# Both key heads of a local-attention block in one unit, and a start from half-width pieces of x, in a two-layer hybrid encoder trunk

## What is computed

```python
h = rms_norm(x, norm_mix)
z = h @ w_in                 # idx/latent, kv, bq, za, zd and 4 x 1024 gate columns
ya = gmlp_mixer(gelu(za))    # A: chunked spatial gating
yb = swa_sink_mixer(...)     # B: 8 query heads on 2 key heads, chunks of 64, window 128, sinks
yc = dsa_mixer(...)          # C: 4 heads over the 64 best keys of an index score
yd = pool_mixer(zd)          # D: causal means over 2, 4, 8, 16 tokens
merged = sum(sigmoid(zg[b]) * (y_b @ w_out[b]) for b in "ABCD")
x = x + merged @ w_o
h2 = rms_norm(x, norm_ffn)
x = x + (silu(h2 @ w_gate) * (h2 @ w_up)) @ w_down
```

## Time and profile before

| | us |
|---|---|
| median of 3 runs | 815.37 (814.8 to 815.8) |
| the profiled execution, its own time | 815.81 |
| its span, first to last instruction | 814.0 |
| PE busy | 805.4 |
| PE weight loads busy | 659.2 |
| DVE busy | 560.1 |
| ACT busy | 405.3 |
| POOL busy | 52.8 |

### The profile page before, as it was taken

The page is one execution under the profiler, slowest core; times in us unless marked ns, Lnnn a source line. Parts: engine busy times, 40 slices in busy tenths (PEclk is TensorE's granted clock), DMA queues, the critical chain, the costliest instruction groups (busy, mean ns, idle before and its releaser), DMA issues.

```text
span 814.0 us, 10244 instructions
## 1 busy us (share of the span) xinstructions
PE 805.4 (99%) x3868; PEld 659.2 (81%) x3868; DVE 560.1 (69%) x844; ACT 405.3 (50%) x558; POOL 52.8 (6%) x103
## 2 busy tenths in 40 slices
PE   7999999999999999999999999999999999999998
PEld 6888777878888888888888887787788888888886
DVE  6898789876576554565568887898675754565443
ACT  6866556454274434444366654755543543444431
POOL 5750000000000000000004100000000000000000
PEclk8999999999999999999999999999999999999999
DMA  8644536635466564665663625474446555666541
GB/s 300 215 147 145 173 135 207 207 127 188 135 223 201 177 191 158 207 205 184 177 218 120 230 82 182 133 252 158 155 155 206 180 183 165 209 196 195 167 155 52
DMA packets 98672, 144.38 MB, mean 177 GB/s; under 512 B 11064, under 2 KB 62016, under 8 KB 98624
## 3 DMA queue, kind: packets, MB, share of 16 engines
q1 hardware_dynamic: 98352, 143.73, 54.2%
q10 hardware_dynamic: 272, 0.00, 0.0%
HBM read 142.54 MB, written 1.05 MB: 176 GB/s over the span
## 4 chain that ended last, share of the span: by engine, by line
PE 95%; SPq 3%; DMA 1%; DVE 0%; ACT 0%; issue 0%; DVEq 0%
PE big L1504 20%; PE big L1508 19%; PE big L1507 19%; PE mix L1508 10%; PE mix L1504 10%; PE mix L1507 10%; SPq L581 2%; PE mix L1873 1%; PE mix L1548 1%; PE mix L1639 1%; DMA w_raw<-in_w_in 1%; PE mix L1572 1%; SPq L526 1%; PE mix L1560 1%; PE mix L1592 1%; PE mix L1625 1%
## 5 line engine op out<-in xcount | busy, mean ns | idle before, releaser
L731 ACT ACTIVATE w_hi<-w_raw 128x2048 fp32r<-128x2048 f32 (+3 forms) x142 | 256.6, 1814 | 163.2 <-DMA w_raw<-in_w_gate_up 88.3
L1032 DVE TENSOR_TENSOR w_lo<-w_raw,w_hi 128x2048 fp32r<-128x2048 f32 (+3 forms) x142 | 306.1, 2172 | 32.9 <-ACT w_hi L731 31.8
L1504 PE MATMUL big<-w_hi,act_hi 128*128 128x512 f32 (+2 forms) x476 | 185.6, 390 | 0.3 <-DVE w_lo L1032 0.3
L1507 PE MATMUL big<-w_lo,act_hi 128*128 128x512 f32 (+2 forms) x476 | 181.7, 382 | 0.0
L1508 PE MATMUL big<-w_hi,act_lo 128*128 128x512 f32 (+2 forms) x476 | 181.6, 382 | 0.0
L1504 PE MATMUL mix<-w_hi,act_hi 128*128 128x512 f32 x352 | 137.5, 391 | 0.0
L1508 PE MATMUL mix<-w_hi,act_lo 128*128 128x512 f32 x352 | 137.2, 390 | 0.0
L1507 PE MATMUL mix<-w_lo,act_hi 128*128 128x512 f32 x352 | 137.1, 389 | 0.0
L1504 PEld LDWEIGHTS big<-w_hi,act_hi 128*128 128x128 f32 x476 | 89.5, 188 | 20.1 <-issue 2.1
L1291 DVE TENSOR_TENSOR y_h_lo<-mix,y_h_hi 128x256 fp32r<-128x256 f32 x44 | 16.6, 419 | 127.4 <-ACT y_h_hi L950 127.4
L1508 PEld LDWEIGHTS big<-w_hi,act_lo 128*128 128x128 f32 x476 | 89.5, 188 | 17.2
(11 more groups left out here) (207 smaller groups left out, 717.2 us busy)
## 6 DMA issues: line engine op xcount, KB each, us to landing
w_raw<-in_w_in SPq DMA_DIRECT2D x44, 1024.0 KB, 5.1
w_raw<-in_w_gate_up SPq DMA_DIRECT2D x88, 512.0 KB, 4.8
w_raw<-in_w_down SPq DMA_DIRECT2D x22, 1024.0 KB, 4.9
w_raw<-in_w_o SPq DMA_DIRECT2D x8, 1024.0 KB, 5.0
w_raw<-in_b_w_out SPq DMA_DIRECT2D x4, 1024.0 KB, 5.9
w_raw<-in_w_in SPq DMA_DIRECT2D x3, 904.0 KB, 4.9
w_raw<-in_w_in SPq DMA_DIRECT2D x4, 512.0 KB, 4.3
w_raw<-in_a_w_out SPq DMA_DIRECT2D x4, 512.0 KB, 3.5
```

What stands on the lines that cost most here:

```text
L731: nc.scalar.activation(high(u)[:, a:b], arrived(u)[:, a:b], ACT.Copy).then_inc(hi_ready, 1)
L1032: nc.vector.tensor_tensor(low(u)[:, a:b], arrived(u)[:, a:b], high(u)[:, a:b].bitcast(F32), ALU.subtract).then_inc(lo_ready, 1)
L1504: ins = nc.tensor.matmul(dst[:, 0:w], xh, wh, start=first and n == 0, stop=False)
L1507: nc.tensor.matmul(dst[:, 0:w], xh, wl, start=False, stop=False)
```

## The change

**Attention.** `ATTN` has four units: B by token block with both key heads, and C by token block. Each unit of B writes 512 columns of each of two score banks where it wrote 256, reduces 1024 scores a row with one instruction, has eight exponentials, and two banks of transposes. `row` is 8 wide, `weights_b` is a view of `probs` with eight heads. In the tables the scores of the first unit move to slot 14, their transposes to 16; the index scores of block 1 move to slot 13 on PE and ACT (DVE's part stays in slot 15), TC to 16 with bank 0, TJ to 17. On DVE softmax_out and softmax_in come ahead of the ydT lows. The sinks are loaded by four DMAs instead of two.

**Start.** x is loaded in four pieces of 128 x 512; unit 1 in two halves as unit 0; the positions by SP. VectorE makes the high part of the first half of units 0 and 1 (`split_high`); ScalarE makes the high activations from PSUM with the gain as its scale (`first_gained`, four instructions of 128x128 for a piece) and VectorE the low ones (`first_low`, four more). Two more products of zeros stand behind the first transposes. The squares of x and their mean move behind slot 1's splits.

```diff
-ATTN = [("B", 0, 0), ("B", 0, 1), ("B", 1, 0), ("B", 1, 1), ("C", 0, 0), ("C", 0, 1)]
+ATTN = [("B", 0), ("B", 1), ("C", 0), ("C", 1)]
...
-    return 1 if ATTN[i][0] == "B" else ATTN[i][2] + 1
+    return 2 if ATTN[i][0] == "B" else ATTN[i][1] + 1
...
-PE_AT = {"latT": 5, "TI": 5, "kv": 7, "wT": 9, "TK": 8, "idx0": 10, "TQ": 11, "idx1": 14, "TC": 15, "TJ": 16,
+PE_AT = {"latT": 5, "TI": 5, "kv": 7, "wT": 9, "TK": 8, "idx0": 10, "TQ": 11, "idx1": 13, "TC": 16, "TJ": 17,
...
-S_AT = [13, 15, 17, 19, 23, 25]
-T_AT = [15, 17, 19, 21, 25, 27]
-Y_AT = [17, 19, 21, 23, 26, 28]
+S_AT = [14, 18, 23, 25]
+T_AT = [16, 20, 25, 27]
+Y_AT = [18, 23, 26, 28]
...
-            def load_tokens(tb):
-                sp.dma_start(xs[:, tb], x[0, tok(tb)]).then_inc(x_in[tb], 16)
+            def load_positions():
+                sp.dma_start(pos_i[:], positions[0].rearrange("(t p) -> p t", p=P),
+                             allow_slow_non_contiguous=True).then_inc(pos_in, 16)
+
+            def load_tokens(tb, h):
+                cols = slice(h * N, (h + 1) * N)
+                sp.dma_start(xs[:, tb, cols], x[0, tok(tb), cols]).then_inc(x_in[tb][h], 16)
...
-                if (l, u) == (0, 0):
+                if l == 0 and u < HALVED:
                     for half, k in ((0, slice(0, 2)), (1, slice(2, 4))):
...
-                        if half == 0:
-                            load_tokens(1)
+                        if (u, half) == (0, 0):
+                            load_tokens(1, 0)
+                        elif (u, half) == (0, 1):
+                            for tb in range(TB):
+                                load_tokens(tb, 1)
+                            load_positions()
...
-                    *((sinks[HD * a:HD * a + HD], b_sinks[l].rearrange("(k a o) -> a k o", k=2, a=2)[a].partition_broadcast(HD))
-                      for a in range(2)),
+                    *((sinks[HD * a:HD * a + HD, o],
+                       b_sinks[l].rearrange("(k a o) -> a o k", k=2, a=2)[a, o].partition_broadcast(HD))
+                      for a in range(2) for o in range(2)),
...
+            def first_gained(tb, h):
+
+                bank = mix_bank("hT", tb, h)
+                act.wait_ge(*mix_is_full(0, "hT", tb, h))
+                for j in range(4):
+                    k = 4 * h + j
+                    e = nc.scalar.activation(act_hi[:, k, tok(tb)], mix[:, bank, j * P:(j + 1) * P], ACT.Copy,
+                                             scale=g_mix[:, k:k + 1])
+                e.then_inc(act_hi_ready.sem, 1)
...
-                    load_positions()
-                    split(0, 0, 0)
-                    high_gained(0, "hT", 0)
+                    act.wait_ge(gain_placed, 1)
+                    first_gained(0, 0)
                     split(0, 0, 1)
-                    high_gained(0, "hT", 1, [0])
-                    x_squares(0, "mix", 0)
-                    split(0, 1, 0)
+                    first_gained(1, 0)
+                    first_gained(0, 1)
+                    first_gained(1, 1)
                     split(0, 1, 1)
-                    high_gained(0, "hT", 1, [1])
-                    x_squares(0, "mix", 1)
...
                     if (l, s) == (0, 1):
+                        for tb in range(TB):
+                            x_squares(0, "mix", tb)
                         tables()
...
+            def first_low(tb, h):
+                bank = mix_bank("hT", tb, h)
+                dve.wait_ge(*act_hi_ready.nth(0, 2 * h + tb + 1))
+                for j in range(4):
+                    k = 4 * h + j
+                    ins = nc.vector.scalar_tensor_tensor(
+                        out=act_lo[:, k, tok(tb)], in0=mix[:, bank, j * P:(j + 1) * P], scalar=g_mix[:, k:k + 1],
+                        in1=act_hi[:, k, tok(tb)].bitcast(F32), op0=ALU.mult, op1=ALU.subtract)
+                ins.then_inc(act_lo_ready.sem, 1)
+                dve.wait_ge(*gained_low(0, "hT", tb, h)).then_inc(mix_drained[bank].sem, 1)
+
+            def split_high(u):
+                dve.wait_ge(first_in[u], 16)
+                nc.vector.tensor_copy(high(u)[:, 0:2], arrived(u)[:, 0:2]).then_inc(first_high, 1)
...
-                    step(l, nc.vector.tensor_reduce(r0, s_in, AX_X, ALU.max))
+                    step(l, nc.vector.tensor_reduce(row[:, 0, :], s_in, AX_X, ALU.max))
...
+                for i in range(len(ATTN)):
+                    if s == T_AT[i] - 1:
+                        softmax_out(l, i)
+                for i in range(len(ATTN)):
+                    if s == S_AT[i]:
+                        softmax_in(l, i)
                 if s == PE_AT["ydT"]:
...
-                    gain_half(0, "hT", 0, 0)
-                    gain_half(0, "hT", 0, 1)
+                    split_high(0)
                     split(0, 0, 0)
-                    gain_low(0, "hT", 0, 0)
-                    gain_half(0, "hT", 1, 0)
+                    first_low(0, 0)
                     split(0, 0, 1)
-                    gain_low(0, "hT", 1, 0)
-                    gain_low(0, "hT", 0, 1)
-                    gain_half(0, "hT", 1, 1)
+                    first_low(1, 0)
+                    split_high(1)
                     split(0, 1, 0)
-                    gain_low(0, "hT", 1, 1)
+                    first_low(0, 1)
+                    first_low(1, 1)
                     split(0, 1, 1)
...
+                    if (l, s) == (0, 1):
+                        mean_of_sums(0, "mix", D_MODEL)
...
-                    turn(l, "hT", 0)
+                    turn(l, "hT", 0, [0])
+                    products_of_zeros(2)
                     first_products(0, 0)
-                    turn(l, "hT", 1)
-                    for half, kind in ((0, 1), (0, 2), (1, 0), (1, 1), (1, 2)):
+                    turn(l, "hT", 1, [0])
+                    for half, kind in ((0, 1), (1, 0), (0, 2), (1, 2), (1, 1)):
                         first_products(half, kind)
+                    for tb in range(TB):
+                        turn(l, "hT", tb, [1])
```

More of the change, by code:

```diff
@@ L154, in mixer_uses @@
              (("TQ", 0), 2), (("TQ", 1), 3), (("spatial",), 1), (("mixed",), 2),
-             (("yaT",), 3), (("S", 0, 0), 0), (("S", 0, 1), 1), (("idx", 1, 0), 0), (("idx", 1, 1), 1),
-             (("ydT", 0), 2), (("ydT", 1), 3), (("TC",), 3)]
-    for i, (m, _, tb) in enumerate(ATTN):
+             (("yaT",), 3), (("idx", 1, 0), 0), (("idx", 1, 1), 1), (("S", 0, 0), 0), (("S", 0, 1), 1),
+             (("ydT", 0), 2), (("ydT", 1), 3), (("TC",), 0)]
+    for i, (m, tb) in enumerate(ATTN):
         if i + 1 < len(ATTN):
@@ L204 @@
            22: (1, 5, 7), 23: (1, 7, 8)}
-DVE_STEPS = 132
+DVE_STEPS = 122
 class Signal:
@@ L320, in trunk_kernel @@
         params_in = signal("params_in", 16 * N_PARAMS)
-        x_in = [sem(f"x_in{tb}") for tb in range(TB)]
+        x_in = [[sem(f"x_in{tb}{h}") for h in range(2)] for tb in range(TB)]
         pos_in = sem("pos_in")
@@ L325, in trunk_kernel @@
         lo_ready = sem("lo_ready")
-        first_in = sem("first_in")
+        first_in = [sem(f"first_in{u}") for u in range(HALVED)]
+        first_high = sem("first_high")
         gain_turned = sem("gain_turned")
@@ L742, in x_squares @@
                 else:
-                    act.wait_ge(x_in[tb], 16)
+                    for h in range(2):
+                        act.wait_ge(x_in[tb][h], 16)
                     for c in range(2):
@@ L846, in exps @@
                         bank = mix_bank("S", i, odd)
-                        for cc in range(2):
-                            h, n = 2 * odd + cc, chunk_keys(tb, cc)
-                            e = nc.scalar.activation(probs[:, h, 0:n], mix[:, bank, cc * P:cc * P + n], ACT.Exp,
+                        for part in range(4):
+                            h, n = 4 * odd + part, chunk_keys(tb, part % 2)
+                            e = nc.scalar.activation(weights_b[:, h, 0:n], mix[:, bank, part * P:part * P + n], ACT.Exp,
                                                      scale=SCALE, bias=row[:, 1, h:h + 1], accum_out=row[:, 4, h:h + 1])
@@ L1229, in softmax_out @@
                     dve.wait_ge(*exp_ready.nth(l, tb + 1))
-                step(l, nc.vector.reciprocal(row[:, 6, :], total))
-                if m == "B" and tb == 0:
-                    parts = [(probs[:, cc::2, 0:chunk_keys(tb, cc)], row[:, 6, cc::2]) for cc in range(2)]
-                else:
-                    n = 2 * CHUNK if m == "B" else keys(tb)
-                    parts = [(probs[:, :, 0:n], row[:, 6, :])]
+                step(l, nc.vector.reciprocal(factor, total))
+                if m == "C":
+                    parts = [(probs[:, :, 0:keys(tb)], factor)]
+                elif tb == 0:
+                    parts = [(weights_b[:, cc::2, 0:chunk_keys(tb, cc)], factor[:, cc::2]) for cc in range(2)]
+                else:
+                    parts = [(weights_b, factor)]
                 for p, r in parts:
@@ L1530, in first_products, with turn @@
```

(14 more changed lines are left out.)

139 lines of the change are left out of this document (70 added, 69 removed).

## The result

The changed kernel takes **819.9 us** (median of 7 runs, 818.9 to 822.5) where the kernel before takes 815.37 (7 runs beside them, 814.1 to 816.0): a ratio of **1.0067, 95% interval 1.0057 to 1.0076** (it follows the means, 820.5 and 815.2, and not the medians). It is slower, by about 5 us.

The account below looks back on a forecast made before the run. TensorE's work and SP's DMA list bound the first 37 us, then TensorE nearly gapless. 815.81 + 1.35 (unit 5) + 2.6 (slot 16) - 0.3 (slot 15) = 819.46, less 0.44 to the median: 819.0 us, range 814.6 to 822.4.

Parts of the forecast that it names:

- Unit 5 later, clock falls: Matmul of unit 5, the second half of the bq weights: 38.4 us for 37.08, +1.35 us; fallen clock only a rival.
- Waits in slot 16: Attention: TensorE waits for softmax_out, queued behind index_scores on VectorE; 1.3 us a layer, +2.6 in all.
- Merged units otherwise: Attention: small gaps of slot 15 go, as its second unit is split earlier; -0.3 us.
- The start: First products: first at 7.8 us for 9.52, stage ends near 21.5 for 22.95; gain about 1.4, between -0.5 and 3.
- SP's list takes it back: DMAs ahead of unit 5: two more sink DMAs cost 1.35 us, range -0.3 to 3.6, whatever the start gained.
- 7.20 + 1.93 + 2.30 stay: From unit 5's issue to its matmul: the transfer of 7.20 us and the splits behind it get no later.
- slack: VectorE ahead of unit 5: waits for ScalarE's split, so its slack is as long as ScalarE's idle 3.83 us.
- Rival (a), the fallen clock,: TensorE stands from 35.2 to 38.4 before unit 5 and its clock falls: 1 to 2.8 us, 820.8; chance 0.26.
- TensorE's matmuls are as many as before: Attention units: unchanged matmul count, twice as many in an S, T or Y of branch B, in half the units.
- DMA issue: Positions moved to SP's queue: costed at nothing, as SP waits at g_lat anyway; 0.6 us more if uncovered.

Follow-up runs that it names:

- e4: The changed kernel with softmax_out ahead of index_scores in VectorE's list: 815.86 us, ratio 1.0015 to the kernel before.
- e10: e8 with idx_w, top8 and row allocated behind all other tiles, so e7 without the merged attention units: 813.03 us, ratio 0.9976 to the kernel before.
- e7: e5 with the last eight parameter DMAs behind unit 5 in SP's list of the first layer: 810.34 us, ratio 0.9940 to the kernel before.
- e3: The changed kernel with row allocated behind all other tiles and a hole of before's size in its place: 817.10 us, ratio 1.0037 to the kernel before.
- e5: e4 with idx_w, top8 and row allocated behind all other tiles: 811.57 us, ratio 0.9957 to the kernel before.
- e6: The kernel before with only idx_w, top8 and row allocated behind all other tiles: 814.02 us, ratio 0.9980.
- e2: The kernel before with the changed attention units alone, including four sink DMAs and the wider row: 820.21 us, ratio 1.0065.
- e1: The kernel before with the changed start alone; attention units, two sink DMAs and row as before: 814.80 us, ratio 0.9999.
- e9: e7 with VectorE's part of unit 5 ahead of its slot 3 steps: 809.99 us, ratio 0.9939 to the kernel before.
- e8: e1 with the last parameter DMAs (g_v, two sinks, w_grp, s_grp, b_sp) behind unit 5 in SP's list: 814.40 us, ratio 0.9989 to the kernel before.

## Why the prediction came out right, and what in it was wrong

The number was good (819.0 forecast, 819.9 measured), the sum behind it less so: **two terms that it lacks, +2.4 to 3.1 and -2.9 us, cancel**, and that they do is luck. By the ratios the loss is 0.0067, 5.5 us:

| Term | forecast, us | measured, us | from |
|---|---|---|---|
| Unit 5 later, clock falls | +1.35 (clock a rival) | +1.1 to +1.8 | the rest of the 5.5, of it about 1.1 the clock (3 of 7 runs, 2.5 us each) |
| Waits in slot 16 | +2.6 | +3.5 in the waits, +4.2 in the time | e4 |
| Merged units otherwise | -0.3 | -2.9 | e10 against e7 |
| Place of y_ac, y_d, y_h | none | +2.4 (e3); +3.1 (4.7 from e4 to e5, less e6's 1.6) | e3, e4 to e6 |

The first row isn't measured but left over. If the waits are booked at the 3.4 us of e4's runs without a fallen clock, it becomes +1.9 to +2.6.

- **The start.** The stage's end was forecast at 21.5 and came at 21.56; the low clock of 8 to 15 us is gone (0.21 us from product to product from 9.75 on, and a clock of 1.00 in each stretch up to 37). But the prediction took its gain of 1.4 us from a single execution, and others with the old start end the stage at 21.77 to 22.74, as shown above. The first product came at 8.62 and not at 7.8: the weights landed before 6.04 (6.9 forecast) and `split_high` took its lower bound (0.63), but the high activations, which the sum left out, held it: ScalarE's first Copy was behind an ACT_TABLE_LOAD of 1.28 us, which before ran at 1.28, ahead of a wait for the weights up to 7.94. It cost nothing at the stage's end, where VectorE's list decides, as the prediction said.
- **"SP's list takes it back"** was the right mechanism with the wrong sizes. Unit 5 was issued at 27.64 (forecast 26.8): the two more sink DMAs cost 2.1 us here and 1.3 in e2, for 1.35, and `w_sp` and `w_ukv` 0.95 more, against a flow that ran 1 us ahead. Not all of the 2.1 is the number of sink DMAs: one of the four took 1.42 us for the others' 0.61 to 0.74, and in e1, with two sink DMAs, `w_grp` took 1.46 for 0.60. But the step "7.20 + 1.93 + 2.30 stay" failed: the transfer took 5.26 us for 7.20, so that the matmul came 0.2 us later and not 1.35. Why the earlier issue of before brought no earlier landing was not tested; issued at 21.42, in e7, unit 5 landed at 28.23. In both kernels the DMA engines moved 9 to 13 GB/s between 27 and 28 us, before unit 5's bytes flowed. e7 and e9 show the third clock behind SP's, VectorE's list, which the prediction had down as slack.
- **Rival (a), the fallen clock,** was no either-or. The profiled run has it (1.6 us: some eight steps of 0.43 for 0.23), and three of the seven runs have the mean clock of 0.998 that goes with it; their mean is 821.9 us against 819.4 for the others. Kernels with the old start can't be counted here, as the low clock in their mean can be that of the start. Runs of 0.998 or less come in e3 (4 of 12), e4 (2 of 12) and e5 (1 of 5) as well, and in none of the 43 runs of e1, e7, e8, e9 and e10, where the profiled gap ahead of unit 5 is 1.4 us or less from start to start. The profiled gap alone doesn't decide: in e3 and e5 it was 2.7 us with the clock at 1.00 all through, and in e4's profiled run, its fastest, it was 1.2 us. The rule of the Trainium skill (TensorE: Matmul & The Clock Gate, Why this matters for your kernels) against long gaps between bursts of matmuls agrees with these runs as a risk and not as a certainty.
- **The wait in slot 16** came where it was forecast, 1.76 and 1.74 us for 1.3. Take the profiled shift of 1.81 us at slot 5 off, and `softmax_out` ends at 107.4, as forecast (107.5); it is TensorE that was early, at 105.75 for 106.2. That half microsecond is part of the merged units' gain, and that part was lost in the wait.
- **"TensorE's matmuls are as many as before", so nothing for the merge.** This step failed. I counted instructions and not the interludes that they lie in, and booked 0.3 us where e10 finds 2.9. The prediction's own slot times had it half (0.9 us less in slots 13 to 15), but as earliness to be lost again.
- **An edit costed at nothing without being named:** `row` from `[P, 8, 4]` to `[P, 8, 8]`. It has no instruction, so it stood in no list.
- **DMA issue.** By the Trainium skill (DMA: Bandwidth & Descriptors, Issuing engines are not separate DMA queues) the positions on SP would cost their issue time and no more. The trace agrees: 0.48 us at 4.33, hidden by the later block at `g_lat` (5.06 us for 5.21).

## What to carry to other kernels

Where TensorE is the chain at 95%, an idea that makes fewer and larger interludes can pay (here -2.9 us) and the kernel still lose, by one call's place in another engine's list and by the size of a scratch tile; so look for the loss before dropping the idea. Put tiles of odd size behind the big ones, and keep TensorE's stationary operands at multiples of 256 bytes from one that is known to be fast: it costs nothing and was worth 1.6 us to the kernel before. A start that is made faster has to be followed through every engine's list up to the first wait that doesn't move; here it took three lists to bring unit 5's matmul from 37.08 to 35.20, and in the time no more than 0.9 us came out (e8; 0.3 by e10 against e6). Before booking what a stage can win, look at more than one execution of it: the old start alone spreads unit 5's matmul over 1.5 us (35.54 to 37.08).

## What the runs showed of the hardware

- **The place of the stationary tile sets the step of matmuls.** For fp32r products of a 128x128 stationary tile and 512 moving columns, the step was 227 to 228 ns with the tile 0 or 256 bytes behind a multiple of 512 from the weight ring, 229 at 192, and 233 at 64 and 320: as if with a period of 256 bytes, by five places. The recorded load of the stationary tile took 188 ns in all, and the page's mean matmul with `y_h` grew by only 2 to 5 ns (390 to 395 for L1507, then L1547), beside rows of 382 to 405; the distance of the starts shows it plainly. Whether the moving operand's place matters too was not tried.
- A sink DMA of 0.5 KB in single elements took 0.6 to 1.7 us of SP's queue (1.66 in e9), in a kernel where plain rows take 0.43; the same four took 2.69 us in e2 and 3.50 in the changed kernel.
- ScalarE loads a table (1.28 us) ahead of its first Copy. In the changed kernel the load starts at 6.08 us, when TensorE has turned x, and delays the Copy; in the kernel before it starts at 1.28 and the Copy waits until 7.94 anyway.
